# Reordering VectorE's, ScalarE's and TensorE's queues at three stage boundaries of a two-block transformer kernel

## The chip, the cores and the metric

One NeuronCore of a Trainium2 chip runs the whole program in one launch. The metric is the device time of an execution in microseconds, and the profile is one further execution taken by the hardware profiler.

## The reference, cut to what matters

The input is 256 tokens of width 2048. A first block has windowed attention with a sink logit beside a gated linear recurrence run in both directions, and then a layer of product-key experts. A second block has a state-space (SSD) mixer and a dilated-attention mixer. The change touches the attention and the recurrence of the first block and the SSD mixer of the second:

```python
s = jnp.where(valid, s, NEG)                       # scores of a head against 256 keys
m = jnp.maximum(jnp.max(s, -1, keepdims=True), sk) # row maximum, and the sink
p = jnp.exp(s - m); p = p / (p.sum(-1) + jnp.exp(sk - m))
h_rec = rg_lru(c, ..., reverse=False) + rg_lru(c, ..., reverse=True)   # two scans
y = gelu(x_gate) * h_rec
...
y = _ssd_chunked(xs * dt, dt * A, Bm, Cm)          # uses exp of differences of cumsum(dt * A)
y = (y + xs * D_skip) * silu(z)
yg = y.reshape(..., SSD_N_GROUPS, -1)              # 8 groups of 512 channels
yg = yg * lax.rsqrt(jnp.mean(jnp.square(yg), -1, keepdims=True) + RMS_EPS)
return (yg * norm_g) @ a_out_w
```

All weights and activations are float32.

## The kernel before, in words

Each engine has its own instruction list, written out by hand in program order, and the lists meet only in semaphores. An engine that waits on a semaphore holds up everything behind it in its list.

Weights stream in tiles of 128x1024 floats, four to a "body" (`STREAM`). SyncE issues the DMA of a tile into a ring of four buffers, ScalarE writes its rounded part `w_hi` (`high`, L1315), and VectorE (`low`, L1850) or GpSimd (`low`, L477, in the gate, up0 and xbc stages) writes the rest `w_lo = raw - w_hi`. TensorE then multiplies three times: w_hi by x_hi, w_hi by x_lo and w_lo by x_hi. A tile of a stage is so worked ahead by four tiles, and `tile_used` gives its buffers free.

**Gate stage.** TensorE goes through 16 half blocks s (`gate_half`), and between them does the attention in eight steps n of four heads: `scores(n)` (L770) after s = 3, 5, 7, 9, 10, 12, 13, 14, `turn_probs(n)` (transposes, L781) two half blocks later, and `values(n)` (L793) one after that. For each step VectorE does `maxima(n)`: the scaled scores plus the mask (L2074), their maximum (L2077), two small operations with the sinks, and the negated maximum (L2080), which releases ScalarE's exponentials `probs(n)`. ScalarE waits for `max_done` in list order, so a late maximum holds up its `high` of the next tile too. VectorE's `head_rows(n)` scales the product. In the same list `gate_work` puts the recurrence: `scan(0)` at s = 2, the product `drive(1)` (L2027) at s = 4, `scan(1)` at s = 6, and the sum of both directions (L2095) at s = 8. Ahead of all of them stands a wait for `sinks_out`, which ScalarE gives after it has copied the turned queries and keys and the sinks. GpSimd does the stage's `w_lo`.

**From xbc to z.** The convolved channels of the SSD mixer end with ScalarE's `convolved_body(23)`, whose last operation is a SiLU. ScalarE then gives `ssd_ready`. TensorE does the first z tile (n = 0), waits for `ssd_ready`, and turns channel group 1 (`turn_group(1)`, L1056). ScalarE makes the decays of head n in `decay_exp(n)`: two ReLU operations on a row of decays (L1692, L1693) and an exponential (L1696). VectorE multiplies them by the masked B C product (`mixed(n)`, L2523), and TensorE's `y_pair(b)` (L1097, L1100) takes heads 2b and 2b + 1 after z tile 2b + 1.

**From z to a_out.** VectorE's list goes by the 64 z tiles n. At n = 62 it subtracts the split of the normalised chunks 0 and 1 (`chunk_low`, L2572). At n = 63 it does `inverted_sum(6)`: scale and shift a group's mean square out of PSUM bank 2 (L2552, gives `sums_out`) and the reciprocal (L2554). After `gate(31)`, `add(31)` and `chunk_sums(7)` it comes to the loop over the 64 a_out tiles, which begins with `norm_chunk(6)` and the split of chunks 2 and 3. ScalarE does the last squares (L1701, `squares(7, 2:4)`, after `y_gated` 32), and then the high parts of chunks 2 and 3 (L1735). TensorE's `norm_tile(i)` uses chunk i of the activations for i below 32. Tile 0 writes PSUM bank 2 in its second half, so it waits there for `sums_out` 7. After tile 3 come the last group's sum (L1074) and `ada_sum("z")` (L922), 24 narrow products over the accumulators that VectorE's `ada_product` (L2278) fills.

Of the kernel before, what the change touches and what calls it, by code (L numbers as in the profile page):

```python
# [7 lines left out]
ALU = mybir.AluOpType  # L8
ACT = mybir.ActivationFunctionType
# [7 lines left out]
P = 128  # L17
S = 256
# [5 lines left out]
LN_EPS = 1e-5  # L24
# [16 lines left out]
SG, SN, SHEADS = 8, 128, 64  # L41
XC = DI // P
BC = XC + 2 * SG
# [106 lines left out]
def build(nc, a, out):  # L150
    ctx = ExitStack()
    with ctx:
# [410 lines left out]
        def _(pe):  # L563
# [539 lines left out]
            for n in range(SHEADS):  # L1103
                g, k = divmod(n, 8)
                h, b = n % 2, n // 2
                if h == 0 and b >= 2:
                    pe.wait_ge(sem("z_taken"), b - 1)
                pe.wait_ge(lo_done, 4 * FIRST_BODY["z"] + n + 1)
                for kk in range(8):
                    w = slice(kk * P, kk * P + P)  # L1110
                    last = three(PS[:, z_bank[b % 2], 0:S], w_hi[:, n % 4, w], w_lo[:, n % 4, w],
                                 xt_hi[:, 8 * h + kk, :], xt_lo[:, 8 * h + kk, :],
                                 h == 0 and kk == 0, h == 1 and kk == 7)
                last.then_inc(tile_used, 1)
                if h:
                    y_pair(b)
                if n == 0:
                    pe.wait_ge(sem("ssd_ready"), 1)
                    pe.wait_ge(dve_free, 2 + DVE_BLOCKS["xbc"] + BC)
                if k == 0 and g + 1 < SG:  # L1120
                    turn_group(g + 1)
                if k == 4 and g + 1 < SG:
                    cb_group(g + 1)
                if k == 6 and g:
                    group_sum(g - 1)
# [183 lines left out]
        def _(act):  # L1309
# [347 lines left out]
            def convolved_body(j):  # L1657
                for u in range(4):
                    if u % 2 == 1:
                        act.wait_ge(tile_used, 4 * j + (4 * FIRST_BODY["xbc"] + u + 1))  # L1660
                        half_out("xbc", 2 * j + u // 2, u // 2).then_inc(sem("half_out"), 1)
                    high(j + (FIRST_BODY["xbc"] + 1), u)
                    if u >= 2:
                        silu(2 * j + (u - 2), u - 2)

# [14 lines left out]
            with act.Fori(8, NB["xbc"]) as j:  # L1680
                convolved_body(j)
            act.wait_ge(sem("conv_read"), BC + 2)
            act.wait_ge(sem("dtn_done"), 1)
            act.sem_inc(sem("ssd_ready"), 1)

            def decay_exp(n):

                act.wait_ge(sem(f"decay_loaded{n % 4}"), 16 * (n // 4 + 1))
                if n >= 4:
                    act.wait_ge(sem("y_product"), n // 2 * 2 - 2)  # L1690
                e, row = ex[:, n % 4, :], decay_rows[:, n % 4, :]
                act.activation(e[:, 0:S], row, ACT.Relu, scale=-1.0, bias=acn[:, 0, n:n + 1])  # L1692
                act.activation(e[:, S:384], row[:, P:S], ACT.Relu, scale=-1.0, bias=acn[:, 1, n:n + 1])\  # L1693
                    .then_inc(sem("decays_read"), 1)
                act.wait_ge(sem("decays_read"), n + 1)
                act.activation(e, e, ACT.Exp, scale=-1.0).then_inc(sem("decays_taken"), 1)  # L1696
# [30 lines left out]
            squares(SG - 1, slice(2, 4), XC).then_inc(sem("group_squared"), 1)  # L1727
            f = FIRST_BODY["a_out"]

            act.wait_ge(tile_used, 4 * f)  # L1730
            for i in range(4 * NB["a_out"]):
                for c in ((2, 3) if i == 0 else (i + 3,)):
                    if c < XC:
                        act.wait_ge(sem("ssd_normed"), c + 1)
                        act.activation(a_hi[:, c, :], xbc[:, c, :], ACT.Copy).then_inc(stage_hi_done, 1)  # L1735
# [108 lines left out]
        def _(dve):  # L1844
# [222 lines left out]
            def maxima(n):  # L2067
                tt, g = steps[n]
                dve.wait_ge(sem("scores_done"), n + 1)
                if n:  # L2070
                    dve.wait_ge(sem("probs_done"), n)
                sinks = PS[:, 7, 4 * g:4 * g + 4]
# [24 lines left out]
            gate_work = {2: lambda: scan(0), 4: lambda: drive(1), 6: lambda: scan(1), 8: both_directions}  # L2097
            dve.wait_ge(sem("sinks_out"), 1)
# [448 lines left out]

            def inverted_sum(g, bank=2):

                dve.wait_ge(sem("group_summed"), g + 1)  # L2550
                o = rg[:, S * g:S * g + S]
                dve.tensor_scalar(o, PS[:, bank, 0:S], 1.0 / 512, LN_EPS, ALU.mult, ALU.add).then_inc(sem("sums_out"), 1)  # L2552
                dve.wait_ge(sem("sums_out"), g + 1)
                dve.reciprocal(o, o).then_inc(sem("root_inverted"), 1)  # L2554
# [21 lines left out]
            for n in range(SHEADS):  # L2576
# [5 lines left out]
                if n == 62:  # L2582
                    chunk_low(0)
                    chunk_low(1)
                if n == 63:
                    inverted_sum(SG - 2)
                low(FIRST_BODY["z"] + n // 4 + 1, n % 4)
                if n % 4:
                    ada_product("z", n // 4, n % 4 - 1, ada_z, ada_acc_z)
# [15 lines left out]
            chunk_sums(SG - 1)  # L2605

# [39 lines left out]
            for i in range(4 * NB["a_out"]):  # L2646
                if i + 6 < XC:
                    norm_chunk(i + 6)
                for c in ((2, 3) if i == 0 else (i + 3,)):
                    if c < XC:  # L2650
                        chunk_low(c)
# [371 lines left out]
```

## Time and profile before

| what | us |
|---|---|
| median of 3 runs | 3255.09 |
| lowest and highest of them | 3254.67, 3256.6 |
| the profiled execution, its own time | 3256.72 |
| its span, first to last instruction | 3255.0 |
| TensorE busy | 3201.7 |
| TensorE's waits for other engines, the longest | 5.5 |
| mean granted clock of TensorE | 0.993 |

The span lies 1.7 us inside the execution's own time. A row of the timeline gives the start, the duration and the instruction, and in brackets the idle time of its engine before it with what ended that. Successive operations overlap by some tenths of a microsecond in the records, so the pace of a chain is read from starts.

### The profile page before, as it was taken

Reading aid. Unit: us, or ns where it says so; the run is one execution under the profiler, and the core shown is the slowest. Engines: PE = TensorE matmul, PEld = TensorE weight load, DVE = VectorE, ACT = ScalarE, POOL = GpSimd, SP = SyncE. Lnnn points to the kernel's source line nnn. Section 1 sums busy time; section 2 is a strip of 40 time slices with the busy share of each in tenths; the row PEclk is TensorE's granted clock in tenths of the full one; section 3 lists DMA queues with packets and bytes.
Section 4 is the critical chain, followed back from the end, with each engine's and each line's share of the span. In section 5 each row is a group of like instructions: output and inputs, shape, how many; then the busy total and the mean of one; then the engine's idle time right before and its main releaser. Section 6 shows DMA issues by size and latency. Waiting matters only on the chain.

```text
span 3255.0 us, 62556 instructions
## 1 busy us (share of the span) xinstructions
PE 3201.7 (98%) x20744; PEld 2870.7 (88%) x20744; DVE 2399.7 (74%) x3930; ACT 1589.7 (49%) x2275; POOL 649.0 (20%) x635
## 2 busy tenths in 40 slices
PE   8999999999999999999999999999999999999997
PEld 8888899999889998899878888888998878888996
DVE  6655569499778997799999775445898877655556
ACT  4755444433453344433444456655766444344443
POOL 1050038200111001100000115886221111100000
PEclk9999999999999999999999999999999999999999
DMA  6435555666787668866655884666776877766444
GB/s 211 148 105 158 174 166 182 189 214 213 248 263 223 213 218 259 266 203 211 199 180 174 269 265 144 188 193 199 240 239 191 290 263 232 251 199 187 149 136 155
DMA packets 185939, 667.84 MB, mean 205 GB/s; under 512 B 24193, under 2 KB 24417, under 8 KB 184529
## 3 DMA queue, kind: packets, MB, share of 16 engines
q1 hardware_dynamic: 149984, 545.91, 53.0%
q0 software_dynamic: 35824, 120.19, 12.2%
q8 instruction: 82, 1.34, 0.2%
q14 instruction: 49, 0.39, 0.0%
HBM read 663.83 MB, written 2.18 MB: 205 GB/s over the span
## 4 chain that ended last, share of the span: by engine, by line
PE 89%; DVE 6%; ACT 3%; issue 2%; DMA 0%; DVEq 0%; ACTq 0%; SPq 0%
PE PS L566 11%; PE PS L568 11%; PE PS L567 11%; PE PS L580 8%; PE PS L957 7%; PE PS L961 7%; PE PS L959 7%; PE PS L581 4%; PE PS L672 2%; PE PS L673 2%; PE PS L674 2%; PE PS L1141 2%; PE PS L1143 2%; PE PS L1145 2%; PE PS L912 1%
## 5 line engine op out<-in xcount | busy, mean ns | idle before, releaser
L1315 ACT ACTIVATE w_hi<-raw 128x1024 fp32r<-128x1024 f32 x1032 | 1091.9, 1059 | 1356.8 <-PE PS L568 614.4
L1850 DVE TENSOR_TENSOR w_lo<-raw,w_hi 128x1024 fp32r<-128x1024 f32 x872 | 1065.0, 1223 | 542.2 <-ACT w_hi L1315 536.9
L566 PE MATMUL PS<-xt,w_hi 128*128 128x256 f32 x2816 | 814.0, 289 | 2.3 <-DVEq L1989 2.1
L567 PE MATMUL PS<-xt,w_hi 128*128 128x256 f32 x2816 | 798.3, 283 | 0.0
L568 PE MATMUL PS<-xt,w_lo 128*128 128x256 f32 x2816 | 798.0, 283 | 0.0
L566 PEld LDWEIGHTS PS<-xt,w_hi 128*128 128x128 f32 x2816 | 541.3, 192 | 11.3 <-issue 10.6
L567 PEld LDWEIGHTS PS<-xt,w_hi 128*128 128x128 f32 x2816 | 541.8, 192 | 0.3
L568 PEld LDWEIGHTS PS<-xt,w_lo 128*128 128x128 f32 x2816 | 541.5, 192 | 0.0
L580 PE MATMUL PS<-xt,w_hi 128*128 128x512 f32 x1320 | 471.8, 400 | 3.8 <-DVE xt L1917 1.4
L477 POOL TENSOR_TENSOR w_lo<-raw,w_hi 128x1024 fp32r<-128x1024 f32 x160 | 391.9, 2466 | 357.4 <-ACT w_hi L1315 229.4
L957 PE MATMUL PS<-w_hi,st_hi 128*128 128x512 f32 x1024 | 401.9, 392 | 0.3
L961 PE MATMUL PS<-w_lo,st_hi 128*128 128x512 f32 x1024 | 398.8, 389 | 0.0
L959 PE MATMUL PS<-w_hi,st_lo 128*128 128x512 f32 x1024 | 398.8, 389 | 0.0
L501 POOL DMA_DIRECT2D ada<-in_ada_w x240 | 129.0, 537 | 1228.3 <-DVE acc_down L2278 632.7
L581 PE MATMUL PS<-xt,w_lo 128*128 128x256 f32 x1320 | 371.1, 281 | 0.0
L580 PEld LDWEIGHTS PS<-xt,w_hi 128*128 128x128 f32 x1320 | 248.6, 188 | 63.6 <-issue 4.5
L581 PEld LDWEIGHTS PS<-xt,w_lo 128*128 128x128 f32 x1320 | 250.0, 189 | 3.5
L957 PEld LDWEIGHTS PS<-w_hi,st_hi 128*128 128x128 f32 x1024 | 192.2, 188 | 40.3 <-ACT hid L1587 1.6
L961 PEld LDWEIGHTS PS<-w_lo,st_hi 128*128 128x128 f32 x1024 | 192.2, 188 | 40.1
L959 PEld LDWEIGHTS PS<-w_hi,st_lo 128*128 128x128 f32 x1024 | 192.3, 188 | 39.0
L2269 DVE TENSOR_REDUCE gate_sum<-PS 128x256 f32<-128x768 f32 x128 | 121.5, 949 | 0.0
L672 PE MATMUL PS<-w_hi,xt 128*128 128x512 f32 x288 | 117.0, 406 | 0.6 <-DVEq L1870 0.6
(427 smaller groups left out, 4613.8 us busy)
## 6 DMA issues: line engine op xcount, KB each, us to landing
raw<-in_u_emb SPq DMA_DIRECT2D x256, 512.0 KB, 3.6
raw<-in_v_emb SPq DMA_DIRECT2D x256, 512.0 KB, 4.4
ada<-in_ada_w POOLq DMA_DIRECT2D x240, 256.0 KB, 4.6
raw<-in_xbc SPq DMA_DIRECT2D x96, 512.0 KB, 3.6
raw<-in_z SPq DMA_DIRECT2D x80, 512.0 KB, 3.7
raw<-in_q SPq DMA_DIRECT2D x64, 512.0 KB, 3.5
raw<-in_a_out SPq DMA_DIRECT2D x64, 512.0 KB, 4.3
raw<-in_k SPq DMA_DIRECT2D x48, 512.0 KB, 4.6
```

The costliest lines, as they stand in the source:

```text
L477: pool.tensor_tensor(w_lo[:, u, :], raw[:, u, :], w_hi[:, u, :].bitcast(F32), ALU.subtract)\
L566: pe.matmul(o, w_h, x_h, start=start, stop=False, skip_group_check=True)
L567: pe.matmul(o, w_h, x_l, start=False, stop=False, skip_group_check=True)
L568: return pe.matmul(o, w_l, x_h, start=False, stop=stop, skip_group_check=True)
L580: pe.matmul(PS[:, b, :], w_h, both, start=k == 0, stop=False, skip_group_check=True)
L581: return pe.matmul(PS[:, b, 0:S], w_l, xt_hi[:, k, :], start=False, stop=False, skip_group_check=True)
L672: pe.matmul(o, source[0][:, k, t], w_hi[:, u, c:c + 512], start=k == 0, stop=False)
L957: pe.matmul(o, st(st_hi, st2_hi, u)[:, t], w_hi[:, u, c], start=start, stop=False, skip_group_check=True)
L959: pe.matmul(o, st(st_lo, st2_lo, u)[:, t], w_hi[:, u, c], start=False, stop=False, skip_group_check=True)
L961: last = pe.matmul(o, st(st_hi, st2_hi, u)[:, t], w_lo[:, u, c], start=False, stop=stop, skip_group_check=True)
L1315: act.activation(w_hi[:, u, :], raw[:, u, :], ACT.Copy).then_inc(hi_done, 1)
L1850: dve.tensor_tensor(w_lo[:, u, :], raw[:, u, :], w_hi[:, u, :].bitcast(F32), ALU.subtract)\
```

## The change

In the gate stage the wait for `sinks_out` moves into `maxima(0)`, and the scans and `drive(1)` stand one half block later in VectorE's list: `scan(0)` after `maxima(0)`, `drive(1)` after `maxima(1)`, `scan(1)` after `maxima(2)`. The sum of both directions stays at s = 8.

Where xbc ends, ScalarE's last body is written out of its loop, and the ReLU operations of heads 0 and 1 (`decay_steps`) stand before its last SiLU. TensorE's wait for `ssd_ready` and `turn_group(1)` move behind z tile 1.

Where a_out begins, VectorE gives `sums_out` 7 at n = 62 between `chunk_low(0)` and `chunk_low(1)` (`sum_scaled`), does `chunk_low(2)` and `chunk_low(3)` at n = 63 ahead of the last z tile's `low`, and moves the reciprocal (`sum_inverted(6)`) and the last two `ada_product`s behind `chunk_sums(7)`. ScalarE makes the high parts of chunks 2 and 3 ahead of the last squares.

```diff
 # TensorE, loop over the 64 z tiles n, after the tile's products
+                if n == 1:
+                    pe.wait_ge(sem("ssd_ready"), 1)
+                    pe.wait_ge(dve_free, 2 + DVE_BLOCKS["xbc"] + BC)
+                    turn_group(1)
                 if h:
                     y_pair(b)
-                if n == 0:
-                    pe.wait_ge(sem("ssd_ready"), 1)
-                    pe.wait_ge(dve_free, 2 + DVE_BLOCKS["xbc"] + BC)
-                if k == 0 and g + 1 < SG:
+                if k == 0 and 0 < g < SG - 1:
                     turn_group(g + 1)
...
 # ScalarE, end of xbc
-            def convolved_body(j):
+            def convolved_body(j, ahead=None):
                 for u in range(4):
...
                     high(j + (FIRST_BODY["xbc"] + 1), u)
+                    if ahead and u == 3:
+                        ahead()
                     if u >= 2:
                         silu(2 * j + (u - 2), u - 2)
+            def decay_steps(n):
+                act.wait_ge(sem(f"decay_loaded{n % 4}"), 16 * (n // 4 + 1))
+                if n >= 4:
+                    act.wait_ge(sem("y_product"), n // 2 * 2 - 2)
+                e, row = ex[:, n % 4, :], decay_rows[:, n % 4, :]
+                act.activation(e[:, 0:S], row, ACT.Relu, scale=-1.0, bias=acn[:, 0, n:n + 1])
+                act.activation(e[:, S:384], row[:, P:S], ACT.Relu, scale=-1.0, bias=acn[:, 1, n:n + 1])\
+                    .then_inc(sem("decays_read"), 1)
+            def first_decay_steps():
+                act.wait_ge(sem("dtn_done"), 1)
+                decay_steps(0)
+                decay_steps(1)
...
-            with act.Fori(8, NB["xbc"]) as j:
+            with act.Fori(8, NB["xbc"] - 1) as j:
                 convolved_body(j)
+            convolved_body(NB["xbc"] - 1, first_decay_steps)
             act.wait_ge(sem("conv_read"), BC + 2)
-            act.wait_ge(sem("dtn_done"), 1)
             act.sem_inc(sem("ssd_ready"), 1)
             def decay_exp(n):
...
+                if n >= 2:
+                    decay_steps(n)
+                e = ex[:, n % 4, :]
                 act.wait_ge(sem("decays_read"), n + 1)
                 act.activation(e, e, ACT.Exp, scale=-1.0).then_inc(sem("decays_taken"), 1)
...
 # ScalarE, start of a_out
+            f = FIRST_BODY["a_out"]
+            def chunk_high(c):
+                act.wait_ge(sem("ssd_normed"), c + 1)
+                act.activation(a_hi[:, c, :], xbc[:, c, :], ACT.Copy).then_inc(stage_hi_done, 1)
+            act.wait_ge(tile_used, 4 * f)
+            chunk_high(2)
+            chunk_high(3)
             squares(SG - 1, slice(2, 4), XC).then_inc(sem("group_squared"), 1)
-            f = FIRST_BODY["a_out"]
-            act.wait_ge(tile_used, 4 * f)
             for i in range(4 * NB["a_out"]):
-                for c in ((2, 3) if i == 0 else (i + 3,)):
...
+                if 0 < i < XC - 3:
+                    chunk_high(i + 3)
                 high(f + 1 + i // 4, i % 4)
...
 # VectorE, gate stage (maxima(n), then the list)
                 if n:
                     dve.wait_ge(sem("probs_done"), n)
+                else:
+                    dve.wait_ge(sem("sinks_out"), 1)
...
-            gate_work = {2: lambda: scan(0), 4: lambda: drive(1), 6: lambda: scan(1), 8: both_directions}
-            dve.wait_ge(sem("sinks_out"), 1)
+            gate_work = {3: lambda: scan(0), 5: lambda: drive(1), 7: lambda: scan(1), 8: both_directions}
...
 # VectorE, z tiles (inverted_sum(g) is now sum_scaled(g, bank) and sum_inverted(g))
                 if n == 62:
                     chunk_low(0)
+                    sum_scaled(SG - 2, 2)
                     chunk_low(1)
                 if n == 63:
-                    inverted_sum(SG - 2)
+                    chunk_low(2)
+                    chunk_low(3)
                 low(FIRST_BODY["z"] + n // 4 + 1, n % 4)
-                if n % 4:
+                if n % 4 and n < 62:
                     ada_product("z", n // 4, n % 4 - 1, ada_z, ada_acc_z)
...
             chunk_sums(SG - 1)
+            sum_inverted(SG - 2)
+            ada_product("z", 15, 1, ada_z, ada_acc_z)
+            ada_product("z", 15, 2, ada_z, ada_acc_z)
...
 # VectorE, a_out tiles
-                for c in ((2, 3) if i == 0 else (i + 3,)):
-                    if c < XC:
-                        chunk_low(c)
+                if 0 < i < XC - 3:
+                    chunk_low(i + 3)
                 if i < 62:
                     low(f + 1 + i // 4, i % 4)
```

## Rows read from the trace of the kernel before

**Rows 1.** The page: busy time of each engine (share of the span) x instructions
```profile
PE 3201.7 (98%) x20744; PEld 2870.7 (88%) x20744; DVE 2399.7 (74%) x3930; ACT 1589.7 (49%) x2275; POOL 649.0 (20%) x635
```

**Rows 2.** TensorE's longest wait (engine, line waited for: us in total, times, longest)
```profile
PE PS L781 <- ACT pr L1469: 5.5, 1, 5.5
```

**Rows 3.** Timeline, TensorE, gate stage (start us, us, what, [idle before <-releaser])
```profile
165.12 1.14 PE L770 MATMUL PS<-kT,qT 64*128 64x256 f32 x8
...
177.74 1.97 PE L781 MATMUL PS<-cc,pr 128*128 128x128 f32 x8 [5.54 <-ACT pr L1469]
...
190.03 1.04 PE L781 MATMUL PS<-cc,pr 128*128 128x128 f32 x8
...
206.52 1.13 PE L770 MATMUL PS<-kT,qT 64*128 64x256 f32 x8
```

**Rows 4.** Timeline, VectorE in the gate stage
```profile
165.44 5.53 DVE L2034 TENSOR_TENSOR_SCAN rr<-aa,ii 128x2048 f32<-128x2048 f32 x1 [3.35 <-ACT PS L1498]
171.01 1.22 DVE L2074 SCALAR_TENSOR_TENSOR sc<-PS,cw 128x1024 f32<-128x1024 f32 x1
...
173.91 1.57 DVE L2080 TENSOR_SCALAR sm<-sm 128x4 f32<-128x4 f32 x1
...
184.72 0.17 DVE L2080 TENSOR_SCALAR sm<-sm 128x4 f32<-128x4 f32 x1
...
187.71 4.42 DVE L2034 TENSOR_TENSOR_SCAN rr<-aa,ii 128x2048 f32<-128x2048 f32 x1
...
197.37 2.28 DVE L2095 TENSOR_TENSOR rr<-rr 128x2048 f32<-128x2048 f32 x1
```

**Rows 5.** Timeline, GpSimd in the gate stage
```profile
166.65 6.50 POOL L477 TENSOR_TENSOR w_lo<-raw,w_hi 128x1024 fp32r<-128x1024 f32 x1
...
173.12 2.33 POOL L477 TENSOR_TENSOR w_lo<-raw,w_hi 128x1024 fp32r<-128x1024 f32 x1
```

**Rows 6.** Two stretches: length, busy of PE PEld DVE ACT POOL, PEclk, DMA, GB/s
```profile
177.70:183.40 5.70, 5.66 (x24) 4.51 (x25) 1.54 (x2) 3.07 (x4) 4.68 (x2) 0.50 0.34 109
...
2485.00:2497.00 12.00, 7.81 (x37) 5.65 (x38) 11.17 (x19) 4.61 (x9) 0.00 (x0) 1.00 0.30 109
```

**Rows 7.** Timeline, ScalarE where xbc ends and z begins
```profile
2257.00 0.51 ACT L1654 ACTIVATE xbc<-cbuf,pc 128x256 f32 x1 [2.47 <-DVEq L2455]
2257.65 0.51 ACT L1692 ACTIVATE ex<-decay_rows,acn 128x256 f32<-128x256 f32 x1
...
2258.47 1.28 ACT L1696 ACT_TABLE_LOAD   x1
...
2261.02 0.52 ACT L1696 ACTIVATE ex<-ex 128x384 f32<-128x384 f32 x1
```

**Rows 8.** Timeline, TensorE at the same place
```profile
2257.63 1.09 PE L1056 MATMUL PS<-cc,xbc 128*128 128x128 f32 x8 [1.68 <-ACTq L1684]
...
2262.24 0.65 PE L1097 MATMUL PS<-ex,xd 128*64 128x256 f32 x4 [0.65 <-DVE ex L2523]
```

**Rows 9.** Timeline, TensorE at the start of a_out
```profile
2485.70 0.50 PE L1141 MATMUL PS<-w_hi,st_hi 128*128 128x512 f32 x1
...
2488.55 0.50 PE L1141 MATMUL PS<-w_hi,st_hi 128*128 128x512 f32 x1 [1.20 <-DVE rg L2552]
...
2495.92 0.47 PE L1141 MATMUL PS<-w_hi,a_hi 128*128 128x512 f32 x1 [2.99 <-DVE a_lo L2572]
...
2501.49 0.59 PE L1074 MATMUL PS<-sq,cc 128*128 128x256 f32 x2
...
2504.59 0.78 PE L1141 MATMUL PS<-w_hi,a_hi 128*128 128x512 f32 x1
```

**Rows 10.** Timeline, VectorE at the start of a_out
```profile
2488.08 0.42 DVE L2552 TENSOR_SCALAR rg<-PS 128x256 f32<-128x256 f32 x1
...
2496.03 1.21 DVE L1850 TENSOR_TENSOR w_lo<-raw,w_hi 128x1024 fp32r<-128x1024 f32 x1
```

**Rows 11.** Timeline, ScalarE at the start of a_out
```profile
2493.23 0.63 ACT L1701 ACTIVATE sq<-xbc 128x512 f32<-128x512 f32 x1 [7.38 <-DVE xbc L2539]
```

## Prediction before the run

> **What bounds the kernel now.** First the page: TensorE is busy for 3201.7 of 3255.0 us [rows 1]. It is the bound nearly everywhere, so an edit on another engine is worth only the part of TensorE's 53 us of idle time that it takes away. Next the list of TensorE's waits: the longest is one wait of 5.5 us for ScalarE's probabilities [rows 2]. Then the timelines around the three places that the change touches. In the gate stage TensorE stands 5.54 us before the first transposes of probabilities, because VectorE did the first scan (165.44, 5.53 us) ahead of the first maxima (171.01) although the scores had been there since 165.12 + 1.14 = 166.26 [rows 3, 4]. At the start of z it waits 1.68 and 0.65 us [rows 8], at the start of a_out 1.20 and 2.99 us [rows 9]. These five are 12.1 us, 0.37% of the time. The two stretches of granted clock say what a wait costs beyond itself: after the 5.54 us the clock stood at 0.50 from 177.7 to 183.4, that is at 1.2 instead of 2.4 GHz, while around the waits of 1.20 and 2.99 us it stayed at 1.00 [rows 6].
>
> **Gate stage.** Nothing is added; three VectorE operations and a wait change places. Without the scan ahead of it the first L2074 starts at about 166.3, since `sinks_out` was given by 165.4 (it is what released the scan) [rows 3, 4]. From the start of L2074 to the start of L2080 are 173.91 - 171.01 = 2.90 us, so L2080 is due at 169.2. It takes 0.17 us alone, but 1.57 us in this first step, and there it ended at 175.48, just when GpSimd's operation of 173.12 + 2.33 = 175.45 did [rows 4, 5]. GpSimd's previous one lasted 6.50 us, from 166.65 over the scan to 173.15 [rows 5]. So one of the two engines stands while the other runs such an operation. Without the scan in its way the 166.65 operation should end after 2.33 us at 169.0, and the next starts there and ends at 171.3. L2080, due 0.2 us after that start, would wait until 171.3. From the end of L2080 to the transposes pass 177.74 - 175.48 = 2.26 us, so these start at 173.6 instead of 177.74. TensorE is free at 177.74 - 5.54 = 172.2: 1.4 us of wait remain, and **4.14 us** go. A wait of 1.4 us is shorter than those that left the clock alone, so the slow stretch goes too: 5.70 us at 0.50 is 2.85 us of work at full clock, **2.85 us** gained [rows 6].
>
> What is late next is VectorE itself, because TensorE now arrives 7.0 us earlier and VectorE's list is as long as it was. I follow it: scan(0) 4.42 us (the second scan's time; the first's 5.53 holds a wait for GpSimd) to 175.8; maxima(1) to L2080 2.90 to 178.7, and two GpSimd operations, the first held up by the scan, end at 175.8 + 2 x 2.33 = 180.5, so L2080 then; `drive(1)` is as large as L2095 and takes 2.28 to 182.8; the probabilities 1 are ready at 180.5 + 2.26 = 182.8, and TensorE wants them at 190.03 - 7.0 = 183.0, no wait [rows 3 to 5]. head_rows(0) follows, three short operations, about 0.8 us (an estimate from L2080's 0.17 and its product of a quarter of L2074's size). The scores 2 come two products after 183.0, at 185.2, maxima(2) is done at 185.2 + 2.90 + 0.2 = 188.3, scan(1) 4.42 to 192.7. Then stand head_rows(1) and L2095, and two GpSimd operations that waited behind the scan may come between: 0.8 + 2.28 + 2 x 2.33 = 7.7, so 200.4. The fourth L2074 ends at 201.6. It reads the scores' bank out, and TensorE's fifth scores need that; by its own work TensorE comes to them at 206.52 - 7.0 = 199.5. That is a new wait of **2.1 us** [rows 3]. Without the two GpSimd operations VectorE would be done at 196.9 and there would be no wait. No row shows L2095 or head_rows against GpSimd; the nearest row is the scan, which like L2095 reads two operands of 128x2048 from SBUF, and I take its behaviour.
>
> On this the Trainium skill, "SBUF — State Buffer", section "Who interferes with whom", has a rule that speaks against the change: a VectorE instruction with two SBUF inputs contends with a GpSimd instruction that reads SBUF, and whichever issues first holds the pair while the other blocks. The scan's row agrees for the scan; no row here shows it for L2095. By the rule the new wait is there, and by the scan's row alone it is likely.
>
> The gate stage gives 4.14 + 2.85 - 2.1 = 4.9 us. Bounds: 5.54 + 2.85 = 8.4 if L2080 slips in ahead of GpSimd and nothing blocks L2095; 2.0 if the fourth probabilities, one scores product and half block behind the late L2074, come late as well and the clock falls once more.
>
> **From xbc to z.** Four ReLUs go ahead of the last SiLU. From the first ReLU to the table load is 2258.47 - 2257.65 = 0.82 us, so two heads are 1.64 us, and before that SiLU ScalarE stands for 2.47 us waiting for VectorE: they are hidden. If that cover were gone they would delay the SiLU, and so all of the boundary, by up to 1.64 us. The ReLU at 2257.65 ran straight after the SiLU, with the table load only behind it, so no load is added; two would cost 2 x 1.28 [rows 7]. The exponential of head 1 at 2261.02 comes 1.64 us earlier, and with it the first `y_pair`, which VectorE's `mixed(1)` releases: 2262.24 becomes 2260.6. TensorE's own work until there is no bound: tile 0 ended at 2257.63 - 1.68 = 2255.95, the tile and the turn take 2262.24 - 0.65 - 2257.63 = 3.96, in either order, so 2259.9 [rows 8]. The first wait vanishes and 0.7 us remain before `y_pair`. Gain **1.65 us**; bounds 0 (the exponential held by its table load) and 1.68 + 0.65 = 2.3. GpSimd's rows of decays for later heads are released earlier, but in its list they stand behind its last `low`, and nothing waits for them here.
>
> **From z to a_out.** Before, two a_out tiles lasted from 2485.70 to 2495.92, 10.22 us; the next two, from 2495.92 to 2501.49, took 5.57 with no wait. If nothing waits **4.65 us** go [rows 9]. Wait one: `sums_out` 7 came from L2552 at 2488.08 + 0.42 and comes now after one `chunk_low`, some 3 us earlier, when bank 2 isn't wanted yet [rows 10]. Wait two: ScalarE stood for 7.38 us ahead of the last squares (from 2485.85 to 2493.23) with the high parts of chunks 2 and 3 behind [rows 11]. They now run at 2485.9. VectorE comes to their low parts at n = 63, after the operations that it did before L2552 at 2488.08 and the 0.4 us of the moved L2552, so by 2488.5, and is done by 2489.3; TensorE wants chunk 2 at 2485.70 + 5.57 = 2491.3. New is that VectorE waits at n = 63 for ScalarE's high parts, with the last `low` of z, the gating and the group's sums behind it in its list; ScalarE has them at 2485.9 + 0.8, so nothing is held. The last squares still wait for the gating, which comes earlier by the 1.7 us reciprocal and a product.
>
> The price is VectorE's lead. Its list between n = 62 and the low part of a_out tile 4 holds the same operations in another order, so that one stays at about 2496.0, done at 2497.2, and the split of chunk 4 follows at 2498.0 after a `norm_chunk` [rows 10]. TensorE came to tile 4 at 2504.59 and comes now at 2504.59 - 4.65 = 2499.9: of a lead of 6.6 us 1.9 remain. The accumulators that `ada_sum` wants at 2501.49 - 4.65 = 2496.8 are done just ahead of `norm_chunk(6)`, at 2495.6. So I count no wait; if VectorE falls behind there, the whole 4.65 could be handed back. Upper bound 4.65 + 1.6: the tiles after `ada_sum` run slowly in both, and might not.
>
> **Sum.** 4.9 + 1.65 + 4.65 = 11.2 us. The profiled execution took 3256.72 (its span 3255.0 and 1.7 around it), which gives 3245.5; the median of the three runs lies 1.6 below it, at 3255.09, so the forecast for the median is **3243.9**.
>
> **Rivals.** A: VectorE hands the gate stage back. At two steps more the maxima come 1.5 to 2 us late behind scans and GpSimd. For it: a lead of 0.2 us at step 1; against it: from the fifth step on VectorE has only maxima and head_rows. The gain of that stage falls to 0.5 or so: 3243.9 + 4.4 = 3248.3. B: the operations don't meet GpSimd. For it: L2080 misses the start of the operation by only 0.2 us, and GpSimd's spans are rough. The gate stage gives 8.4: 3240.4. C: TensorE waits for VectorE in a_out from tile 4 on, the lead of 1.9 us being used up: 4.65 back, 3248.6. For it: VectorE's split, `low`, norm and product a tile leave little; against it: the lead exists. D, slower: the many short waits of the gate stage each let the clock fall. Each is some 1.7 us and a slow stretch of 2.85 us, 4.55 together, against 8.4 + 1.65 + 4.65 = 14.7 to be gained, so from the fourth such wait on the kernel is slower; with all eight steps 3255.09 + 8 x 4.55 - 14.7 = 3276.8. Against it: the waits of 1.20 and 2.99 us left the clock at 1.00.
>
> **How the numbers follow.** Forecast 0.53 (its own range 3241.5 to 3246.5), A 0.19, B 0.13, C 0.10, D 0.05. Two tenths of a per cent, 6.5 us, is about what a measurement of this kernel can tell from no change; faster by more than that means below 3248.6. All of the forecast and of B lie there, and half of A and C: 0.81. Slower by more than that is most of D, 0.04, and the rest is 0.15. The range reaches from B, 3239.5, to the far side of A and C, 3250.
>
> **What would show it.** Right: the wait before the first L781 falls from 5.54 to some 1.4 us, the clock keeps 1.00 there, and a new wait of some 2 us stands before the fifth L770; L1056 has no wait and the first L1097 stands 4.7 us after the end of z tile 0; the first four a_out tiles follow each other in 11.1 us. Wrong: a granted clock of 0.50 anywhere else in the gate stage, waits of TensorE for `w_lo` or `a_lo` after tile 3, or a table load among the last SiLUs.

## The result, and the profile of the changed kernel

| | median us | repeats | lowest to highest | ratio to before, 95% |
|---|---|---|---|---|
| before | 3255.09 | 5 | 3254.65 to 3259.01 | |
| changed | 3240.69 | 5 | 3239.07 to 3241.39 | 0.9950 [0.9939, 0.9960] |
| before, measured again | 3256.68 | 13 | 3255.10 to 3259.15 | |
| changed, measured again | 3244.77 | 5 | 3240.99 to 3245.79 | 0.9961 [0.9947, 0.9974] |

The forecast was 3243.9 us, with 3241.5 to 3246.5 as its own range; the first median, 3240.69, lies 0.8 us below that range. It is 14.4 us faster than before, 3.2 more than the sum of 11.2. The same kernel measured again came out 11.9 us faster. What lies between the two is the subject of the experiments. First the three stages.

The profiled execution took 3239.50 us, its span 3237.8. The page: TensorE is busy for 8.4 us less than in [rows 1].

```profile
PE 3193.3 (99%) x20744; PEld 2865.1 (88%) x20744; DVE 2403.1 (74%) x3930; ACT 1589.1 (49%) x2275; POOL 642.2 (20%) x635
```

TensorE's waits (line waited for: us in total, times, longest). The wait of [rows 2] is 1.5 us long, a new one of 1.0 stands at L770, and L1056 and the first tiles of a_out are no longer in the list. The five waits of the prediction were 12.1 us and are 3.1 (1.49, 0.96 and 0.69, below); that is 8.9 of the span's 17.2 us, and the 8.4 us of busy time are nearly all the rest.

```profile
PE PS L1097 <- DVE ex L2544: 1.6, 4, 0.7
PE PS L781 <- ACT pr L1470: 1.5, 1, 1.5
...
PE PS L770 <- DVE sc L2096: 1.0, 1, 1.0
```

The gate stage on VectorE, which answers to [rows 4] (L2074, L2080, L2034, L2095 are now L2096, L2102, L2054, L2117). The maxima run at once, and the scan behind them. L2102 (the negation), L2108 (the first operation of `head_rows`) and L2117 (`both_directions`) have a long and a short form: 2.17, 1.46 and 0.17 us for the negation of 128x4 numbers.

```profile
166.37 1.23 DVE L2096 SCALAR_TENSOR_TENSOR sc<-PS,cw 128x1024 f32<-128x1024 f32 x1 [4.27 <-PE PS L770]
...
169.27 2.17 DVE L2102 TENSOR_SCALAR sm<-sm 128x4 f32<-128x4 f32 x1
171.35 4.41 DVE L2054 TENSOR_TENSOR_SCAN rr<-aa,ii 128x2048 f32<-128x2048 f32 x1
...
178.86 1.46 DVE L2102 TENSOR_SCALAR sm<-sm 128x4 f32<-128x4 f32 x1
180.23 2.28 DVE L2047 SCALAR_TENSOR_TENSOR ii<-ii,rr 128x2048 f32<-128x2048 f32 x1
...
188.46 0.17 DVE L2102 TENSOR_SCALAR sm<-sm 128x4 f32<-128x4 f32 x1
188.54 4.42 DVE L2054 TENSOR_TENSOR_SCAN rr<-aa,ii 128x2048 f32<-128x2048 f32 x1
192.99 2.15 DVE L2108 TENSOR_TENSOR sm<-sm 128x4 f32<-128x4 f32 x1
...
195.73 3.89 DVE L2117 TENSOR_TENSOR rr<-rr 128x2048 f32<-128x2048 f32 x1
199.66 1.23 DVE L2096 SCALAR_TENSOR_TENSOR sc<-PS,cw 128x1024 f32<-128x1024 f32 x1
```

GpSimd's operations beside them, against [rows 5]: the long forms of the 128x4 operations end when one of these ends (171.41, 195.11), and L2117 starts while the third runs.

```profile
169.02 2.39 POOL L477 TENSOR_TENSOR w_lo<-raw,w_hi 128x1024 fp32r<-128x1024 f32 x1
...
191.86 3.25 POOL L477 TENSOR_TENSOR w_lo<-raw,w_hi 128x1024 fp32r<-128x1024 f32 x1 [3.58 <-ACT w_hi L1316]
...
195.09 2.39 POOL L477 TENSOR_TENSOR w_lo<-raw,w_hi 128x1024 fp32r<-128x1024 f32 x1
```

TensorE in the same stage, against [rows 3]. The stage ends with L845, which came at 245.42 before; counted from the first L770 (165.13, before 165.12) the stage is 74.96 us long, against 80.30.

```profile
173.70 1.09 PE L781 MATMUL PS<-cc,pr 128*128 128x128 f32 x8 [1.49 <-ACT pr L1470]
...
183.41 1.03 PE L781 MATMUL PS<-cc,pr 128*128 128x128 f32 x8
...
200.94 1.13 PE L770 MATMUL PS<-kT,qT 64*128 64x256 f32 x8 [0.96 <-DVE sc L2096]
...
240.09 3.84 PE L845 MATMUL PS<-diag,qn 128*128 128x128 f32 x32 [0.19 <-DVE diag L1945]
```

From xbc to z: ScalarE, then TensorE (against [rows 7, 8]). The ReLUs stand ahead of the last SiLU, which still waits 0.95 us for VectorE, and one table load follows. L1056 has no wait, and 0.69 us are left at L1097.

```profile
2245.59 0.50 ACT L1675 ACTIVATE ex<-decay_rows,acn 128x256 f32<-128x256 f32 x1
...
2248.02 0.51 ACT L1655 ACTIVATE xbc<-cbuf,pc 128x256 f32<-128x256 f32 x1 [0.95 <-DVEq L2476]
2248.63 1.28 ACT L1711 ACT_TABLE_LOAD   x1
```

```profile
2249.90 1.04 PE L1056 MATMUL PS<-cc,xbc 128*128 128x128 f32 x8
2251.63 0.65 PE L1097 MATMUL PS<-ex,xd 128*64 128x256 f32 x4 [0.69 <-DVE ex L2544]
```

The start of a_out on TensorE, against [rows 9]: four tiles without a wait from 2475.10 to 2486.11, 11.01 us. The x24 group is the run of narrow products (one column each) of `ada_sum`.

```profile
2475.10 0.50 PE L1142 MATMUL PS<-w_hi,st_hi 128*128 128x512 f32 x1
...
2486.11 0.59 PE L1074 MATMUL PS<-sq,cc 128*128 128x256 f32 x2
2486.54 2.73 PE L922 MATMUL PS<-cc,ada_acc_z 128*128 128x1 f32 x24
```

Comparing both kernels at marks ahead of and behind each stage, the gate stage gave 5.3 us, xbc to z 1.7 (the first L1056, at 2228.99 before, comes 8.9 us early, the first L1097 10.6), a_out 4.8 (its first product comes 10.6 us early, L1074 15.4). That is 11.8. The end of the span is 17.2 us earlier. The other 5.4 lie where nothing was changed. They show in the granted clock around the runs of narrow products: up2, up3, the step product, a_out, behind k2 and late in v2 (columns: stretch, length, busy us of the engines, PEclk, DMA, GB/s). First the kernel before:

```profile
1012.00:1030.00 18.00, 17.81 (x148) 17.61 (x148) 15.35 (x25) 4.78 (x6) 1.07 (x2) 0.91 0.58 168
1390.00:1409.00 19.00, 18.81 (x162) 18.57 (x160) 16.36 (x27) 5.17 (x8) 1.07 (x2) 0.91 0.55 171
1976.00:1996.00 20.00, 20.00 (x132) 18.32 (x131) 5.16 (x12) 9.45 (x14) 10.91 (x5) 0.91 0.35 106
2485.00:2512.00 27.00, 22.81 (x108) 18.39 (x109) 23.57 (x38) 10.11 (x16) 1.60 (x3) 0.94 0.49 156
2803.00:2830.00 27.00, 26.42 (x146) 22.86 (x145) 15.62 (x19) 8.95 (x13) 3.76 (x7) 0.94 0.77 247
2870.00:2895.00 25.00, 25.00 (x117) 20.92 (x116) 10.54 (x13) 9.28 (x9) 0.00 (x0) 0.93 0.55 166
```

Then the changed kernel, with the stretch of [rows 6] ahead, now at full clock:

```profile
177.70:183.40 5.70, 5.70 (x51) 5.70 (x50) 5.47 (x8) 3.05 (x10) 2.58 (x2) 1.00 0.60 183
...
1012.00:1030.00 18.00, 18.00 (x169) 17.91 (x168) 16.81 (x30) 5.96 (x8) 1.61 (x3) 1.00 0.67 206
1390.00:1409.00 19.00, 19.00 (x164) 18.91 (x163) 16.43 (x30) 5.77 (x8) 1.61 (x3) 0.91 0.62 188
1976.00:1996.00 20.00, 20.00 (x131) 18.07 (x130) 6.14 (x15) 10.60 (x14) 11.08 (x5) 1.00 0.44 133
2485.00:2512.00 27.00, 27.00 (x134) 22.72 (x133) 26.62 (x43) 14.32 (x21) 4.84 (x9) 1.00 0.76 245
2803.00:2830.00 27.00, 26.42 (x125) 22.20 (x125) 14.80 (x16) 8.79 (x10) 3.22 (x6) 0.94 0.69 219
2870.00:2895.00 25.00, 25.00 (x118) 20.83 (x119) 10.94 (x12) 9.82 (x11) 0.00 (x0) 0.93 0.50 153
```

A mean of 0.91 over 18 us is 18 x 0.09 = 1.6 us of lost work, one stretch of 3.4 us at 1.2 instead of 2.4 GHz. The kernel before has one at each of the six places, the changed kernel at three. Three times 1.7 us are 5.1 of the missing 5.4. Theory: which places meet such a stretch differs from execution to execution, and the change has no part in it. Rival: the change removes them.

### The profile page after: what moved, and what is told of

The parts are those of the page before. It is cut to its first block, busy times and chain, and to the rows that moved or that the text cites. A ratio compares the mean times of both kernels' runs of the same rounds, so it can differ in the third digit from the quotient of the medians.

```text
span 3237.8 us, 62549 instructions
## 1 busy us (share of the span) xinstructions
PE 3193.3 (99%) x20744; PEld 2865.1 (88%) x20744; DVE 2403.1 (74%) x3930; ACT 1589.1 (49%) x2275; POOL 642.2 (20%) x635
## 4 chain that ended last, share of the span: by engine, by line
PE 89%; DVE 6%; ACT 3%; issue 2%; DMA 0%; DVEq 0%; ACTq 0%; SPq 0%
PE PS L566 11%; PE PS L568 11%; PE PS L567 11%; PE PS L580 8%; PE PS L957 7%; PE PS L959 7%; PE PS L961 7%; PE PS L581 4%; PE PS L672 2%; PE PS L674 2%; PE PS L673 2%; PE PS L1142 2%; PE PS L1144 2%; PE PS L1146 2%; PE PS L912 1%
## 5 line engine op out<-in xcount | busy, mean ns | idle before, releaser
L477 POOL TENSOR_TENSOR w_lo<-raw,w_hi 128x1024 fp32r<-128x1024 f32 x160 | 385.4, 2426 | 356.6 <-ACT w_hi L1316 228.6
```

Source lines behind the costliest of these rows:

```text
L477: pool.tensor_tensor(w_lo[:, u, :], raw[:, u, :], w_hi[:, u, :].bitcast(F32), ALU.subtract)\
```

## The parts of the change, one at a time

Each kernel is the one before with one part of the change alone.

**e1_gate.** The order of scans and maxima:

```diff
-            gate_work = {2: lambda: scan(0), 4: lambda: drive(1), 6: lambda: scan(1), 8: both_directions}
-            dve.wait_ge(sem("sinks_out"), 1)
+            gate_work = {3: lambda: scan(0), 5: lambda: drive(1), 7: lambda: scan(1), 8: both_directions}
```

> Only the gate stage's edit, on the kernel before. Theory (parts plus slow stretches): the stage ends 5.3 us earlier, as in the changed kernel, with a wait of 1.5 us ahead of the first L781 and 1.0 us ahead of the fifth L770; everything behind it falls 5.3 us earlier against the moments at which the clock is granted, so some of the six half-clock stretches behind the narrow products (L922) may go or come, 1.7 us each. Time 3255.1 - 5.3 = 3249.8, give or take 1.7 us a stretch (3244.7 to 3251.5). Rival (stretches go because a wait before them goes): the stretches at 1024, 1403, 1990, 2505, 2826 and 2891 us all stay, since nothing near them changes, and the time is 3249.8 within 0.7 us.

Measured 3250.23 against 3256.43 us, ratio 0.998 [0.997, 0.9989]. The waits ahead of the first L781 and the fifth L770 are 1.51 and 0.96 us. Of the six stretches the one near 1024 is gone and the one near 1990 is twice as long, so the rival, by which all stay, is out, though the time fits it.

**e2_turn.** The four ReLUs ahead of the last SiLU and the turn ahead of the first `y_pair`:

```diff
+            convolved_body(NB["xbc"] - 1, first_decay_steps)
...
+                if n == 1:
...
+                    turn_group(1)
```

> Only the edit where xbc ends (first decays ahead of the last SiLU, the turn behind z tile 1). Theory: 1.7 us from the first y_pair on; nothing before 2255 us differs, so the stretches at 1024, 1403 and 1990 us are those of the kernel before if a program always meets the granted clock at the same moments, and may differ if it meets it at others from execution to execution. Time 3255.1 - 1.7 = 3253.4, 3.4 less or 1.7 more with the stretches behind it. Rival: the exponentials are held by their table load and the gain is 0.

Measured 3254.32, ratio 0.9994 [0.9985, 1.0003]: the median is 2.1 us lower, no difference that the interval can tell from none. The stretch near 1990 is gone, ahead of anything that this edit touches.

**e3_aout.** The splits of chunks 2 and 3 ahead of the last squares, the group's sum taken out early:

```diff
+            chunk_high(2)
+            chunk_high(3)
             squares(SG - 1, slice(2, 4), XC).then_inc(sem("group_squared"), 1)
...
+                    sum_scaled(SG - 2, 2)
...
+                    chunk_low(2)
+                    chunk_low(3)
```

> Only the edit where a_out begins. Theory: the first four tiles follow each other without a wait, 4.8 us earlier; the half-clock stretch behind the narrow products of that place may go or stay, 1.7 us. Time 3255.1 - 4.8 = 3250.3, or 3248.6 where the stretch goes. Rival 1 (the stretch goes because the waits of 1.20 and 2.99 us before it go): the stretch at the place is gone in the profile, those at 1024, 1403 and 1990 us stay, and the time is 3248.6. Rival 2 (VectorE's lead is used up): a wait of TensorE for a_lo or w_lo after tile 3, and 3253 or more.

Measured 3249.61, ratio 0.9978 [0.9969, 0.9987]. The stretch at the place itself stays (0.94), although the waits ahead of it are gone, so rival 1 is out; no wait comes after tile 3, so rival 2 is too.

The three differences are 6.2 + 2.1 + 6.8 = 15.1 us, each 0.4 to 2 us above its stage's shift. That the parts don't work on each other is better read from the profiles: the gate stage is 75.00 us long in e1_gate and 74.96 in the changed kernel, from the first L1056 to the first L1097 are 31.41 us in e2_turn and 31.51 there (33.25 before), and the first four a_out tiles take 11.03 us in e3_aout and 11.01 there. The slow stretches are not the same: up to 2480 us e3_aout runs the code of the kernel before, yet it shows 1.00 in 1976:1996 where before shows 0.91. The same code met the slow clock in one execution and not in another.

## The narrow products spread out

**e4_spread.** The changed kernel, with the twelve narrow products (24 instructions) of each of the six places put one by one between wide ones; for up2 and up3 (`step` issues the next narrow product):

```diff
-                ada_sum(f"down{quarter - 2}", 3, acc_down)
+            spread_body(0, 2 * quarter - 2,
+                        (lambda: ada_parts(f"down{quarter - 2}", 3, acc_down)) if quarter > 1 else None)
...
+                        step(parts if 8 * h + k < 15 else None)
```

> The changed kernel, with the narrow products (12 matmuls with one column each, five places) put one by one between the wide products of the next tile, instead of one after the other. The same products, none added. Theory: half-clock stretches belong to those runs of narrow products and fall on them or not by the moment; spread out they leave no stretch at all, so the three of the changed kernel's profile (1396, 2809, 2874 us) go: 3 x 1.7 = 5.1 us, 3240.7 - 5.1 = 3235.6, and the executions lie closer together than 2.3 us. Rival (the stretches have another cause, or a narrow product between wide ones costs TensorE more than in a run): the granted clock keeps its stretches, or the products cost 0.1 us each more, 60 x 0.1 = 6 us, and the time is 3240 to 3247.

(The expectation counts five places; the run late in v2, near 2873, is a sixth.) Measured 3243.93 (3243.41 to 3245.17), ratio 0.9962 [0.9948, 0.9975]: in the rival's range, and not faster than the changed kernel. At five places the clock stayed at 1.00. Behind k2 it did not: the run had covered a wait for the norm's halves there. TensorE's row of that wait, and the granted clock behind it:

```profile
2806.30 0.50 PE L682 MATMUL PS<-w_hi,xt 128*128 128x512 f32 x1 [3.15 <-DVEq L1922]
```

```profile
2806.00:2821.00 15.00, 14.70 (x49) 12.55 (x50) 2.16 (x3) 1.06 (x1) 0.54 (x1) 0.54 0.35 97
```

Where the changed kernel waits 0.58 us and runs slowly for 3.4, this one waits 3.15 and runs slowly for 13.7. That costs 2.6 + 5.1 = 7.7 us and takes back most of what five places can give, 5 x 1.7 = 8.5. Whether the longer wait or the narrow products among the wide ones keep the clock down so long wasn't tried apart.

**e7_spread2.** The same, but behind k2 the run stays in one piece with six spare wide products in it:

```diff
-            ada_sum("a_out", 3, ada_acc_a)
+            for n, _ in enumerate(ada_parts("a_out", 3, ada_acc_a)):
+                if n % 2:
+                    spare_products(1, 5)
```

(The expectation names four places; the run late in v2 was spread in it as well.)

> After the change, with the twelve narrow products of the sums over partitions put one by one between wide products at four places (second blocks of up2 and up3, the step product, the fifth tile of a_out), and at the fifth (behind k2) left together with six spare wide products between them. Theory (the half-clock stretches of 3.4 us stand behind runs of narrow products and cost 1.7 us each; which of them appear differs between executions of one code): no stretch at the four places in any execution, so the repeats of this kernel lie closer together than the changed kernel's 2.3 us, and the time is the changed kernel's less 0 to 3 us, 3237 to 3240; the stretches near 2808 and 2873 may remain. Rival (the stretches come from the fillings and waits at these places and not from the narrow products): stretches remain at two or more of the four places, time 3240 to 3243.

Measured 3236.06 (3235.72 to 3239.21), ratio 0.9940 [0.9926, 0.9953]: 1.00 at all five spread places, 0.94 behind k2. The time is below the expected 3237. The expectation that its repeats lie closer together failed (3.5 us against 2.3). One cost came in: the run of 2.73 us no longer stands ahead of tile 4 of a_out, and TensorE waits 0.66 us there for VectorE's `a_lo`. That is the lead of 1.9 us that the prediction had worked out, used up.

**e9_after_again, e10_before_spread, e11_spread2_again**, on one chip: the changed kernel unaltered, the kernel before with the spreading of e7_spread2, and e7_spread2 itself.

> The changed kernel once more, unaltered. Theory (which half-clock stretches an execution meets is a matter of chance, and the profiled one met few): the time lies with the runs that had two or three of the four stretches, 3241 to 3244, and the profile shows another set of them than the first. Rival (the change itself removes them): 3239 to 3241.5, and the profile shows the same single one of the four, near 1395 us.

> The kernel before, with its narrow products spread among wide ones at the same four places (and the run behind k2 as in e7_spread2), nothing of the change. Theory: all four of its stretches at these places (near 1023, 1402, 1989 and 2504 us) go, at 1.7 us each: 3249 to 3251.5. What the change does without them is then this kernel less the changed one with the same spreading: 11.8 us by the three stages' shifts, 11 to 13.5. Rival (the change removes the stretches by itself, spreading has no price to save in the kernel before): 3255 to 3257, and the difference is 18 to 20.

> The changed kernel with the narrow products spread at four places, once more, beside the two others on one chip. Theory: 3236 again, no stretch at the four places. Rival: another set of stretches and 3238 to 3241.

Measured, with 3256.68 for the kernel before: 3244.77 (ratio 0.9961 [0.9947, 0.9974]), 3247.87 (0.9973 [0.9964, 0.9983]) and 3236.31 (0.9938 [0.9925, 0.9952]). The first lies 0.8 us above its theory's range and the second 1.1 below, the third where it was expected. The six places in the changed kernel's second profile:

```profile
1012.00:1030.00 18.00, 18.00 (x169) 17.91 (x168) 16.92 (x30) 6.11 (x8) 1.61 (x3) 1.00 0.67 201
1390.00:1409.00 19.00, 19.00 (x164) 18.91 (x164) 16.28 (x30) 6.12 (x8) 1.61 (x3) 0.91 0.63 182
1976.00:1996.00 20.00, 20.00 (x113) 17.94 (x111) 3.39 (x8) 9.45 (x13) 7.62 (x4) 0.83 0.28 90
2485.00:2512.00 27.00, 27.00 (x119) 22.50 (x118) 25.62 (x40) 13.99 (x21) 3.78 (x7) 0.87 0.61 182
2803.00:2830.00 27.00, 26.42 (x134) 22.43 (x133) 14.91 (x18) 9.02 (x10) 3.23 (x6) 0.94 0.70 217
2870.00:2895.00 25.00, 25.00 (x125) 21.11 (x124) 10.56 (x11) 9.39 (x9) 0.00 (x0) 1.00 0.59 172
```

The program is the same, the set is another: the stretches at 1976 and 2485 are back, twice as long, the one at 2870 is gone. Two places without narrow products differ as well. Near 47 and near 1960 us TensorE has just waited 2.1 and 1.43 us, in both profiles alike. First the first profile, then the second:

```profile
40.00:55.00 15.00, 12.92 (x95) 12.72 (x95) 10.94 (x20) 4.24 (x4) 0.00 (x0) 0.89 0.53 173
1955.00:1966.00 11.00, 9.32 (x57) 7.81 (x57) 9.98 (x22) 8.71 (x19) 0.00 (x0) 1.00 0.26 88
...
40.00:55.00 15.00, 12.90 (x108) 12.70 (x107) 12.40 (x21) 4.24 (x4) 0.00 (x0) 1.00 0.56 185
1955.00:1966.00 11.00, 9.32 (x46) 7.71 (x46) 9.56 (x21) 8.89 (x18) 0.00 (x0) 0.84 0.17 50
```

Counting a double stretch twice, the first profile has four and the second seven; three more at 1.7 us are 5.1 of the 5.3 us by which its span is longer (3243.1 against 3237.8). The other executions of this program go the same way: of all ten, those with a mean granted clock of 0.996 have spans of 3237.4 and 3237.8 us, those with 0.995 of 3239.0 to 3241.0, those with 0.994 of 3243.1 to 3244.1. The gate stage took 75.00 us, as in the first profile (74.96), so that gain is firm and the clock's is not. Over all profiles, the granted clock of the six stretches:

| kernel | up2 | up3 | step | a_out | k2 | v2 |
|---|---|---|---|---|---|---|
| before | .91 | .91 | .91 | .94 | .94 | .93 |
| changed | 1 | .91 | 1 | 1 | .94 | .93 |
| changed, again | 1 | .91 | .83 | .87 | .94 | 1 |
| e1_gate | 1 | .91 | .83 | .94 | .94 | .93 |
| e2_turn, e3_aout (alike) | .91 | .91 | 1 | .94 | .94 | .93 |
| e5_neg | 1 | .91 | .91 | 1 | .94 | .93 |
| e6_both | .91 | .91 | .91 | 1 | .94 | .93 |
| e4_spread | 1 | 1 | 1 | 1 | .75 | 1 |
| e7_spread2, e11 (alike) | 1 | 1 | 1 | 1 | .94 | 1 |
| e8_best | 1 | 1 | 1 | 1 | .87 | 1 |
| e10_before_spread | 1 | 1 | 1 | .94 | 1 | 1 |

At the five places other than k2 the unspread runs met a slow stretch in 29 of 40 cases, the spread ones in 1 of 25. That one, in e10, stands right behind the 2.98 us wait of [rows 9], so a wait of this size can cost a stretch too. Three shorter runs of narrow products, 16 instructions in 1.84 us and spread in no kernel, met none in all 13 profiles. The place near 1960 was slow in four of the eight unspread profiles and in none of the five others, though nothing was spread there; why is open.

The places are not alike. Up3 was slow in all eight unspread profiles. Up2 was slow in before, e2_turn, e3_aout and e6_both, and at full clock in both profiles of the changed kernel, in e1_gate and in e5_neg. So for step, a_out and v2 one program is shown with and without the stretch; for up2 it isn't, and a part of the change in its 1.7 us, by moving the moment, isn't excluded.

What the change is worth nearly without them comes from the spread kernels. The kernel before gains 8.8 us from spreading, the changed one 3244.77 - 3236.31 = 8.5. And with the narrow products spread in both, the change is worth 3247.87 - 3236.31 = 11.6 us. The rival, with 18 to 20, is out.

## VectorE against GpSimd in the gate stage

**e5_neg.** The changed kernel, the negation with one input in PSUM:

```diff
-                dve.tensor_scalar(sm[:, n, 0, :], sm[:, n, 0, :], -1.0, None, ALU.mult).then_inc(sem("max_done"), 1)
+                dve.tensor_tensor(sm[:, n, 0, :], sm[:, n, 1, :], sinks, ALU.subtract).then_inc(sem("max_done"), 1)
```

> After the change, with the negated maximum taken as (sinks minus maximum) minus sinks, so that one input stands in PSUM; the result is the same number. Theory (a VectorE instruction that reads SBUF alone is held while GpSimd's instruction runs): the negations before the second and third chunk of gate pieces fall from 2.17 and 1.46 us to about 0.16 each, TensorE's 1.49 us wait for the probabilities goes, and the gate stage ends about 1.5 us earlier than in the changed kernel: ratio to the kernel before about 0.9945. Rival (the negation is long for a reason of its own, for instance the queue ahead of it): it stays near 2 us, and the time equals the changed kernel's, ratio 0.995.

Measured 3243.23 (3241.58 to 3249.80), ratio 0.9964 [0.9950, 0.9977], not the 0.9945 of the theory and no difference from the changed kernel that the spread can tell. VectorE in the gate stage:

```profile
167.78 0.16 DVE L2102 TENSOR_TENSOR sm<-sm,PS 128x4 f32<-128x4 f32 x1
167.85 6.37 DVE L2054 TENSOR_TENSOR_SCAN rr<-aa,ii 128x2048 f32<-128x2048 f32 x1
...
177.23 3.67 DVE L2047 SCALAR_TENSOR_TENSOR ii<-ii,rr 128x2048 f32<-128x2048 f32 x1
180.94 2.22 DVE L2108 TENSOR_TENSOR sm<-sm 128x4 f32<-128x4 f32 x1
...
197.83 1.23 DVE L2096 SCALAR_TENSOR_TENSOR sc<-PS,cw 128x1024 f32<-128x1024 f32 x1
```

Half of the theory holds: the negation takes 0.16 us and the 1.49 us wait at L781 is gone. But the hold only moves on, to the scan (6.37 for 4.41), the drive (3.67 for 2.28) and L2108 (2.22 for the 0.16 of 182.54 us in the changed kernel). From the first to the fourth L2096 VectorE's list takes 32.95 us (from 164.88), against 33.29. TensorE comes 1.7 us sooner and waits 2.33 us at the fifth L770, and now the clock falls:

```profile
199.10:202.40 3.30, 3.29 (x14) 2.48 (x15) 2.36 (x7) 1.48 (x6) 0.00 (x0) 0.53 0.03 11
```

The stage becomes 75.85 us long, 0.9 more than in the changed kernel.

**e6_both.** `both_directions` one place later:

```diff
-            gate_work = {3: lambda: scan(0), 5: lambda: drive(1), 7: lambda: scan(1), 8: both_directions}
+            gate_work = {3: lambda: scan(0), 5: lambda: drive(1), 7: lambda: scan(1), 9: both_directions}
```

> After the change, with the sum of both directions one place later in the gate work (behind the fourth first maxima). Theory (the 1.0 us wait of TensorE before the fifth score product is for VectorE's scaled scores, which stand behind this sum): the wait goes and the gate stage ends 1.0 us earlier; with four or five half-clock stretches at will the whole is 3239 to 3241. Rival: the wait only moves to the head rows that now stand behind the sum, no change.

Measured 3241.18 (3240.05 to 3243.55), ratio 0.9954 [0.9940, 0.9968]. The median is 0.2 us above the expected range. The 0.96 us wait is gone, as expected, and the stage is 73.70 us long, 1.3 less; the sum then takes 2.28 us instead of 3.89.

**e8_best.** e5_neg, e6_both and e7_spread2 in one kernel.

> The three edits of the runs with the negation, the moved sum and the spread narrow products at once. Theory: they add up, 1.5 + 1.0 + 0 to 3 us less than the changed kernel, 3235 to 3238. Rival (each only shifts the wait to the next instruction, or the spread products hold the clock down): 3240 to 3243.

Measured 3234.70 (3232.84 to 3236.43), ratio 0.9931 [0.9917, 0.9945]: the fastest kernel here, 21.9 us under the one before. It is 1.4 under e7_spread2, which the two intervals can't tell from none. The gate stage is 71.89 us long, 3.1 less than in the changed kernel, more than the two edits give by themselves (+0.9 and -1.3). With the sum out of the way, the time that the negation saves doesn't come back as a wait. The profile gives no shorter span than e7_spread2's, 3234.8 against 3234.4 us: it has a slow stretch near 47 us that e7_spread2's lacks, and one behind k2 that is twice as long, which cost 2 x 1.7 = 3.4 us.

## Why the prediction was right, and where it was wrong

**Gate stage: 4.9 forecast, 5.3 measured.** The wait fell by 5.54 - 1.49 = 4.05 (4.14 forecast), the clock kept 1.00, and the new wait came at the fifth L770, as worked out, with 0.96 us for 2.1. Its parts are in the rows: L2117 was held for 3.89 - 2.28 = 1.6 us and L2108 for 2.0, 3.6 together, where I had put two GpSimd operations of 2.33. These parts make 4.05 + 2.85 - 0.96 = 5.9. Most of the 0.6 us to the measured 5.3 can be read from the rows: from the first to the second L781 pass 190.03 - 177.74 = 12.29 us before and 183.41 - 173.70 = 9.71 after, so the clock gave back 2.6 and not 2.85, and behind the fifth L770, 5.58 us early, another 0.25 are lost by L845. That L2117 behaves like the scan, for which no row stood, is now shown. The Trainium skill, "SBUF — State Buffer", section "Who interferes with whom", agrees with these rows: two inputs in SBUF contend with a GpSimd operation that reads SBUF. e5_neg agrees with its other side: with one of its two inputs in PSUM the operation isn't held. That the negation was held with a single input goes with the section's remark that `tensor_scalar` can enter modes that use both ports; no run shows in which mode it ran.

**xbc to z: 1.65 forecast, 1.7 measured.** The ReLUs were hidden, no table load was added, and 0.69 of the 0.7 us remained ahead of L1097.

**a_out: 4.65 forecast, 4.8 measured.** Both waits went, the four tiles took 11.01 us (11.1 forecast), and no wait came at tile 4. The lead of 1.9 us was enough, and about that size: e7_spread2, where the run of 2.73 us no longer stands ahead of that tile, waits 0.66 us there.

**Rivals.** A's waits behind the fifth step didn't come, B's free run of the operations past GpSimd didn't either, C's wait is not in the list, and D's clock stayed up in the gate stage. In e5_neg, as D has it, the clock fell at a 2.33 us wait there. The first median is close to B's 3240.4, but that is a coincidence: the operations did meet GpSimd.

**What failed** is the sum. 4.9 + 1.65 + 4.65 has no term for the clock outside the gate stage: that was put at nothing, without a reason. The one word on it is "Upper bound 4.65 + 1.6: the tiles after `ada_sum` run slowly in both, and might not". I took the half-clock stretches for a fixed part of the kernel, equal in both, with one of them as a doubt. In the first pair of profiles three of them, 5.1 us, are there before and not after. Two of the three, at step and a_out, are back in the second profile of the same program, so they are no fixed part of the code and the change didn't remove them; for the third, at up2, a part of the change stays possible.

The terms themselves came out at 5.3 + 1.7 + 4.8 = 11.8, against 11.2. The second measurement, 3244.77 us and 11.9 faster than before, lies in the range, and with the narrow products spread the change is worth 11.6. That these two come so close is in part luck, since each holds a few stretches of its own. What was missing is the spread that belongs around any such sum: the five places alone can move an execution by 5 x 1.7 = 8.5 us.

Why the five executions of the first measurement all fell on the low side stays open. Executions measured together may share something that decides it. Which chip they ran on is not on record, and the later measurements come from two chips, so a difference between chips isn't excluded either.

## What to carry to other kernels

Before a difference of a few us is put down to an edit, compare the granted clock at places that the edit doesn't touch, and take more than one profile: stretches that come and go between executions of one program aren't part of the change. Put one-column products between wide ones, but look first at what wait a run of them covers. Where an engine's list was the bound, freeing one operation of a hold by another engine moved the hold to the next one; the wait went only where work left the list ahead of it.

## What the runs showed of the hardware

- A VectorE operation on 128x4 numbers took 0.16 us or up to 2.2, by whether a GpSimd operation of 2.3 us ran; with one input in PSUM it took 0.16 in each step.
- Around the end of a 2.73 us run of narrow products the clock fell to 1.2 GHz for 3.4 us, in some cases 6.8, in some executions and not at all in others, at three places of one program. Such runs met a slow stretch in 29 of 40 cases, the same products spread among wide ones in 1 of 25.
- A wait of 2.1 us near 47 us, and one of 1.43 near 1960, were followed by a slow stretch in one execution of a program and not in another.
- Narrow products put among wide ones behind a wait of 3.15 us left the clock at 1.2 GHz for 13.7 us, where the run of them, with a wait of 0.58 us behind it, cost 3.4 us.
